# Gate vectors of the first layer on VectorE, and weight buffers with a 32-byte offset for some panels

## The chip, the cores and the metric

The kernel runs on one core of one Trainium2 chip. The metric is the device time of one execution in microseconds (us), the median of several runs. TensorE multiplies matrices, VectorE and ScalarE work on elements, GpSimd helps a little, and the queue of SyncE (SP) starts most transfers from HBM to SBUF.

## What is computed

The reference is two blocks, one behind the other, over a context of 256 tokens and a latent part of 256 tokens, each token with 1024 features, in float32.

```python
def reference(x, c, ctx, c_ctx, w_ada, b_ada, ...):
    x = first_block(x, c, ctx, c_ctx, w_ada, b_ada, g_attn, w_in, ...)
    return second_block(x, c_2, ctx_2, c_ctx_2, ada_w_2, ada_b_2, ...)
```

The first block has two layers. Each takes a modulated norm, projects it (`w_in`) into gates, latent queries and keys, and a neighbourhood attention, runs the two attentions, multiplies both by sigmoid gates, and goes through `w_out` and a feed-forward part with squared relu (`w_ff1`, `w_ff2`). The second block has two layers of one mixer each, an mLSTM and an attention with a band and a sink. In every layer shift, scale and gate vectors come from the condition: `silu(c) @ ada_w + ada_b`, for latent and context tokens. These products of a vector and a matrix are the "ada vectors".

## The kernel before

**Weights as panels.** All weights come in panels of at most 2176 columns on 128 partitions, in one order (`plan`, `items`). Most hold 8 slices of 256 columns, 1 MB. A panel is loaded into one of three raw slots (`raw`, a ring: the transfer of a panel waits until the panel before it in the slot has been used). ScalarE copies it, rounded to fp32r, into `whi` (line 1368) and VectorE writes the remainder `raw - whi` into `wlo` (line 2010), each in two halves. There are two buffers of each, so a panel's copy waits until TensorE has used the panel before the last. Activations are kept as such pairs too (XAh and XAl, and more). Each product is three fp32r matmuls: hi x hi, hi x lo, lo x hi (lines 624 to 626, and 653 to 655, 700 to 702, 718 to 720, 736 to 738 in the other forms). In `weight_left`, `weight_late`, `weight_pair` and `weight_four` the panel is the stationary operand (128 columns of it) and the activations stream, 512 columns for both token parts or 256 for one. In `tokens_left` and `tokens_half` the activations are stationary and the panel streams. A panel of 8 slices and 256 columns against 512 tokens is 2 x 8 x 3 = 48 matmuls.

**Order.** Each engine has its own program, written out by hand and in order. TensorE calls `weights(p)` and `rest(p, k)`, which wait for the first and the second half of the remainder. `begin(p)` on ScalarE and VectorE makes the hi part and the remainder of the next panel. In the gates of a layer (VectorE lines 2372 to 2395) there are four panels for each of four heads h: gm and gn (gates, 48 matmuls each in the first layer), mo and no (outputs of the two attentions, 4 slices, 24 matmuls each). VectorE multiplies the gates in, adds, and writes the remainder for the next product.

**The ada vectors.** Each vector is a row of 1024 values out of four ada panels (`ADA`, index i, four to a vector r = i // 4), each of two slices of 1024 columns. `AFTER` and `WITH` say behind which panel each stands. An ada panel uses its raw slot only. If i is not in `SUMMED`, TensorE does the product itself: `ada(i)`, 8 fp32 matmuls with 32 output partitions (line 781), each of them two records in the trace. If i is in `SUMMED`, VectorE does it (`vector_part`, line 2042): two slices, for latent and context, so four operations of 1024 columns, a product where a vector begins and a multiply-add otherwise (lines 2000 and 2005). TensorE then only adds the partitions up: `vector_sums(r)` (line 793), behind the last panel of the vector. `rows_out` moves the finished row into columns: two transposes on TensorE (line 803) and one addition on VectorE. `vector_part` stands ahead of `begin` for the same panel on VectorE, and calls `rows_out` for the second panel of a vector. Its first panel also waits for TensorE's sum of the vector before, since both use `parts_of`.

**Where tensors lie.** SBUF is allocated in the order of the program, and each tensor takes a multiple of 32 bytes per partition. The first ones (constants, small vectors, ones) end on a multiple of 64, and three of one column each (line 360) move what follows to 32 past it. So XAh, XAl, the raw slots, `whi` and `wlo` (4 x 2176 bytes each, a multiple of 64) begin at a remainder of 32 modulo 64, as every slice of a panel does. `scale1` (line 373) has 8 columns, 32 bytes, and everything behind it begins at a remainder of 0: MHL and NHL (inputs of mo and no), gYh and gYl (of wo), H (of ff2), lYh and lYl (of mw), aYh and aYl (of atw), and ckh and ckl (of ukv). Behind `gq8` (another 32 bytes) cqh and cql, the partners of uq, are at 32 again.

## Time and profile before

| | |
|---|---|
| median of 3 runs | 2008.11 us (2007.9 to 2010.7) |
| the profiled execution, its time | 2010.52 us |
| its span, first to last instruction | 2008.7 us |
| TensorE (PE) busy | 98% of the span |
| VectorE (DVE) busy | 63% |
| ScalarE (ACT) busy | 45% |
| granted clock of TensorE, mean | 0.999 |
| read from HBM | 274 MB |

The rows further down come from one profiled execution. Times are from the start of its span. PE is TensorE's matmuls, PEld its weight loads, which run beside them. A row of a matmul gives its own length with the tail of the pipeline, and the next one starts before it ends. L626 is line 626 of the kernel. In `t` and `ps` are SBUF and PSUM.

### The profile page before, as it was taken

To read this page: it belongs to the slowest core of one execution; us is meant where nothing else is said; L and a number is where in the kernel's file an instruction comes from. 1 tells how busy PE (TensorE), PEld (TensorE's weight loads), DVE (VectorE), ACT (ScalarE), POOL (GpSimd) and SP (SyncE) were. 2 spreads that over 40 slices of the span, in tenths; PEclk is the share of its full clock that TensorE was granted. 3 is DMA by queue.
4 is the path that set the end of the run, shared out by engine and by line. 5 is a ranking of instruction groups with operands and counts; after the bars stand their busy time and mean duration, and the time that the engine had idled before them with its cause. 6 is when DMAs were issued, how large, how long until landed. Compare 5 with 4: busy or idle time off the path is not lost.

```text
span 2008.7 us, 30598 instructions
## 1 busy us (share of the span) xinstructions
PE 1973.0 (98%) x12332; PEld 1649.3 (82%) x12332; DVE 1266.4 (63%) x2375; ACT 905.1 (45%) x1635; POOL 52.1 (3%) x78
## 2 busy tenths in 40 slices
PE   7999999999999999999999999999999999999998
PEld 5788777779878787899689899998887787888877
DVE  5447764546877565566665777675655464555886
ACT  4446762234423231355664554443444432234675
POOL 0000000001000000000000000000000000001000
PEclk9999999999999999999999999999999999999999
DMA  7322016443454545342129455554321133332411
GB/s 307 116 97 72 17 42 230 169 157 126 149 207 171 207 169 208 146 164 105 53 94 341 174 189 179 181 183 168 105 74 53 43 126 126 137 136 84 140 50 43
DMA packets 53580, 278.34 MB, mean 139 GB/s; under 512 B 4536, under 2 KB 19128, under 8 KB 24512
## 3 DMA queue, kind: packets, MB, share of 16 engines
q1 hardware_dynamic: 47168, 265.50, 36.5%
q10 hardware_dynamic: 6128, 10.03, 1.6%
q8 instruction: 98, 1.61, 0.3%
q0 software_dynamic: 144, 0.85, 0.1%
q14 instruction: 42, 0.34, 0.1%
HBM read 274.26 MB, written 2.11 MB: 138 GB/s over the span
## 4 chain that ended last, share of the span: by engine, by line
PE 84%; DVE 10%; ACT 3%; issue 1%; DMA 1%; POOL 0%; SPq 0%; ACTq 0%; DVEq 0%
PE ps L624 16%; PE ps L626 16%; PE ps L625 16%; PE ps L842 3%; DVE t L2010 3%; DVE t L1996 3%; PE ps L736 3%; PE ps L738 3%; PE ps L737 3%; PE ps L874 2%; PE ps L861 2%; PE ps L1234 2%; PE ps L655 2%; PE ps L653 2%; PE ps L654 2%
## 5 line engine op out<-in xcount | busy, mean ns | idle before, releaser
L624 PE MATMUL ps<-t 128*128 128x512 f32 (+1 forms) x1936 | 669.0, 346 | 3.1 <-DVE t L2010 3.1
L626 PE MATMUL ps<-t 128*128 128x512 f32 (+1 forms) x1936 | 662.6, 342 | 0.0
L625 PE MATMUL ps<-t 128*128 128x512 f32 (+1 forms) x1936 | 662.3, 342 | 0.0
L2010 DVE TENSOR_TENSOR t<-t 128x1024 fp32r<-128x1024 f32 (+2 forms) x370 | 414.2, 1160 | 197.8 <-ACT t L1368 196.9
L1368 ACT ACTIVATE t<-t 128x1024 fp32r<-128x1024 f32 (+3 forms) x376 | 357.9, 999 | 199.3 <-PE ps L626 142.9
L624 PEld LDWEIGHTS ps<-t 128*128 128x128 f32 x1936 | 365.3, 189 | 56.7 <-issue 5.9
L626 PEld LDWEIGHTS ps<-t 128*128 128x128 f32 x1936 | 365.3, 189 | 44.7
L625 PEld LDWEIGHTS ps<-t 128*128 128x128 f32 x1936 | 365.4, 189 | 43.9 <-issue 0.7
L1996 DVE TENSOR_TENSOR t<-t 128x256 f32<-128x256 f32 (+9 forms) x622 | 227.0, 386 | 141.5 <-ACT t L1740 38.1
L2005 DVE SCALAR_TENSOR_TENSOR t<-t 128x1024 f32<-128x1024 f32 (+6 forms) x340 | 234.0, 717 | 36.0 <-ACT t L1473 21.6
L1473 ACT ACTIVATE t<-ps 128x512 f32<-128x512 f32 (+2 forms) x239 | 113.6, 494 | 296.2 <-PE ps L626 198.4
L2005 DVE SCALAR_TENSOR_TENSOR t<-ps,t 128x256 f32<-128x256 f32 (+3 forms) x184 | 84.8, 483 | 133.9 <-PE ps L626 91.7
L736 PE MATMUL ps<-t 128*128 128x256 f32 (+2 forms) x524 | 158.6, 303 | 1.2 <-issue 0.7
L738 PE MATMUL ps<-t 128*128 128x256 f32 (+2 forms) x524 | 152.0, 290 | 0.0
L737 PE MATMUL ps<-t 128*128 128x256 f32 (+2 forms) x524 | 151.9, 290 | 0.0
L1996 DVE TENSOR_TENSOR t<-ps,t 128x128 fp32r<-128x128 f32 (+6 forms) x140 | 53.1, 383 | 94.6 <-ACT t L1862 34.1
L736 PEld LDWEIGHTS ps<-t 128*128 128x128 f32 x524 | 100.0, 191 | 6.9 <-issue 2.8
L737 PEld LDWEIGHTS ps<-t 128*128 128x128 f32 x524 | 100.1, 191 | 4.0 <-issue 2.4
L738 PEld LDWEIGHTS ps<-t 128*128 128x128 f32 x524 | 100.1, 191 | 1.4
L1496 ACT ACTIVATE t<-ps,t 128x512 f32<-128x512 f32 (+1 forms) x128 | 87.1, 697 | 10.5 <-DVE t L1996 10.5
L842 PE MATMUL ps<-t 64*128 64x512 f32 (+3 forms) x256 | 79.6, 571 | 0.6 <-ACT t L1473 0.6
L1485 ACT ACTIVATE t<-ps 128x1024 f32<-128x1024 f32 x56 | 57.5, 1027 | 45.9 <-PE ps L861 45.9
(191 smaller groups left out, 2349.9 us busy)
## 6 DMA issues: line engine op xcount, KB each, us to landing
t<-in_panels SPq DMA_DIRECT2D x231, 1024.0 KB, 4.9
t<-in_panels SPq DMA_DIRECT2D x12, 768.0 KB, 4.4
t<-in_panels SPq DMA_DIRECT2D x16, 512.0 KB, 4.0
t<-in_window ACTq DMA_DIRECT2D x4, 768.0 KB, 4.3
t<-gates_between ACTq DMA_DIRECT2D x4, 512.0 KB, 5.0
t<-in_panels SPq DMA_DIRECT2D x1, 1088.0 KB, 5.0
t<-in_ctxT SPq DMA_DIRECT2D x1, 1024.0 KB, 6.9
t<-in_xT SPq DMA_DIRECT2D x1, 1024.0 KB, 9.1
```

Of the source, the lines that this page charges most:

```text
L624: e.matmul(o, hi[:, k, w], xh[:, c0:c1], start=k == 0, stop=False)
L625: e.matmul(o, hi[:, k, w], xl[:, c0:c1], start=False, stop=False)
L626: t = e.matmul(o, lo[:, k, w], xh[:, c0:c1], start=False, stop=k == p.nk - 1)
L736: e.matmul(o, xh[:, r], hi[:, k, n0:n1], start=k == 0, stop=False)
L737: e.matmul(o, xh[:, r], lo[:, k, n0:n1], start=False, stop=False)
L738: t = e.matmul(o, xl[:, r], hi[:, k, n0:n1], start=False, stop=k == p.nk - 1)
L842: t = e.matmul(o[g][:, x * w:x * w + w], u["q"][g][x], u["k"][g], start=True, stop=not u["mask"])
L1368: e.activation(p.half(whi[p.buf], a), p.half(raw[p.slot], a), ACT.Copy).then_inc(*up(se, ("hi", p.i, a)))
L1473: e.activation(o, i, func, scale=scale).then_inc(*up(se, ("read", key), *names))
L1996: e.tensor_tensor(o, a, b, op).then_inc(*up(ve, *names))
L2005: e.scalar_tensor_tensor(o, a, s_, b, o1, o2).then_inc(*up(ve, *names))
L2010: e.tensor_tensor(p.half(wlo[p.buf], a), p.half(raw[p.slot], a), p.half(whi[p.buf], a).bitcast(F32), ALU.subtract).then_inc(*up(ve, ("lo", ...
```

## The change

Two things change. First, `GATES` lists gm, gn and mo of each head once, with one ada panel behind each, and all twelve (ada panels 8 to 19, the vectors 2 to 4 of the first layer) are in `SUMMED`. Before, only those behind gm were (8, 11, 14, 17), two stood behind most gn, and TensorE did the other eight. Second, `whi` and `wlo` have 2304 columns instead of 2176, and a panel's split parts begin `first_column(key)` columns in, 8 columns (32 bytes) for the panels that the function lists and 0 for the others. The raw slots stay as they are. All places that read or write `whi` and `wlo` go through `split`.

```diff
-GATES = [("gm", 0, 0), ("gn", 0, 0), ("gn", 0, 0), ("gm", 0, 1), ("gn", 0, 1), ("gn", 0, 1), ("gm", 0, 2), ("gn", 0, 2), ("mo", 0, 2),
-         ("gm", 0, 3), ("gn", 0, 3), ("gn", 0, 3)]
+GATES = [(kind, 0, h) for h in range(4) for kind in ("gm", "gn", "mo")]
...
-SUMMED = {AT_START + n for n, key in enumerate(AFTER) if key in MLP_PANELS[3:29] or len(key) == 2 or key[:2] == ("gm", 0)}
+SUMMED = {AT_START + n for n, key in enumerate(AFTER) if key in MLP_PANELS[3:29] or len(key) == 2 or key in GATES}
...
+def first_column(key):
+    kind, l, n = key[0], key[1], key[-1]
+    if kind in ("uq", "mv") or kind == "na" and n >= 4:
+        return 8
+    if (kind == "ukv" or kind in ("mo", "no") and len(key) == 3 and l == 0 or kind == "wo" and l == 0 and n < 3
+            or kind == "ff2" and l == 0 and n < 15 or kind == "mw" and n < 7):
+        return 8
+    if kind in ("cq", "ckv", "gm", "gn", "ff1") and l == 1 or kind == "ff1" and n < 2 or kind == "mq" and n < 2 or kind == "atz":
+        return 8
+    return 0
+
+
+WCOLS = 2304
...
+        self.first = 0 if self.whole else first_column(key)
+
+    def split(self, pair):
+        return pair[self.buf][:, self.first:self.first + self.nk * self.n]
...
-        whi = [sb([128, PCOLS], F32R) for _ in range(2)]
-        wlo = [sb([128, PCOLS], F32R) for _ in range(2)]
+        whi = [sb([128, WCOLS], F32R) for _ in range(2)]
+        wlo = [sb([128, WCOLS], F32R) for _ in range(2)]
...
-                hi, lo = p.view(whi[p.buf]), p.view(wlo[p.buf])
+                hi, lo = p.view(p.split(whi)), p.view(p.split(wlo))
...
-                    e.activation(p.half(whi[p.buf], a), p.half(raw[p.slot], a), ACT.Copy).then_inc(*up(se, ("hi", p.i, a)))
+                    e.activation(p.half(p.split(whi), a), p.half(raw[p.slot], a), ACT.Copy).then_inc(*up(se, ("hi", p.i, a)))
...
-                e.tensor_tensor(p.half(wlo[p.buf], a), p.half(raw[p.slot], a), p.half(whi[p.buf], a).bitcast(F32),
+                e.tensor_tensor(p.half(p.split(wlo), a), p.half(raw[p.slot], a), p.half(p.split(whi), a).bitcast(F32),
                                 ALU.subtract).then_inc(*up(ve, ("lo", p.i, a)))
```

## Rows read from the trace of the kernel before

**Rows 1.** The page: TensorE's busy time, and the chain by engine.
```profile
PE 1973.0 (98%) x12332; PEld 1649.3 (82%) x12332; DVE 1266.4 (63%) x2375; ACT 905.1 (45%) x1635; POOL 52.1 (3%) x78
...
PE 84%; DVE 10%; ACT 3%; issue 1%; DMA 1%; POOL 0%; SPq 0%; ACTq 0%; DVEq 0%
```
**Rows 2.** Timeline (start us, us, instruction): first matmuls of ff1 (0,7) and its successor.
```profile
554.14 0.39 PE L624 MATMUL ps<-t 128*128 128x512 f32 x1
...
565.02 0.40 PE L653 MATMUL ps<-t 128*128 128x512 f32 x1
```
**Rows 3.** Timeline: first matmuls of ff2 (0,7) and its successor.
```profile
690.89 0.39 PE L624 MATMUL ps<-t 128*128 128x512 f32 x1
...
702.09 0.40 PE L624 MATMUL ps<-t 128*128 128x512 f32 x1
```
**Rows 4.** Timeline: two matmuls of ukv of the first layer, twelve apart.
```profile
155.59 0.40 PE L736 MATMUL ps<-t 128*128 128x512 f32 x1
...
158.39 0.40 PE L736 MATMUL ps<-t 128*128 128x512 f32 x1
```
**Rows 5.** Timeline: first matmuls of ff1 (1,5) and its successor.
```profile
1165.90 0.28 PE L624 MATMUL ps<-t 128*128 128x256 f32 x1
...
1171.66 0.28 PE L624 MATMUL ps<-t 128*128 128x256 f32 x1
```
**Rows 6.** Timeline: first matmuls of ff2 (1,9) and its successor.
```profile
1283.14 0.28 PE L624 MATMUL ps<-t 128*128 128x256 f32 x1
...
1288.80 0.28 PE L624 MATMUL ps<-t 128*128 128x256 f32 x1
```
**Rows 7.** Timeline: first and last matmul of na (1,4), whose panel streams.
```profile
940.44 0.28 PE L736 MATMUL ps<-t 128*128 128x256 f32 x1
...
951.82 0.28 PE L738 MATMUL ps<-t 128*128 128x256 f32 x1
```
**Rows 8.** Timeline: a matmul and the weight load of the next one.
```profile
372.04 0.39 PE L624 MATMUL ps<-t 128*128 128x512 f32 x1
372.04 0.19 PEld L625 LDWEIGHTS ps<-t 128*128 128x128 f32 x1
```
**Rows 9.** Timeline of TensorE: ada blocks between panels of the first layer's gates.
```profile
303.63 0.39 PE L626 MATMUL ps<-t 128*128 128x512 f32 x1
303.94 1.95 PE L781 MATMUL ps<-t 128*32 128x256 f32 x32
305.82 0.50 PE L624 MATMUL ps<-t 128*128 128x512 f32 x1
306.16 0.39 PE L625 MATMUL ps<-t 128*128 128x512 f32 x1
...
375.53 1.07 PE L781 MATMUL ps<-t 128*32 128x256 f32 x16
376.42 1.05 PE L793 MATMUL ps<-t 128*32 128x256 f32 x16
```
**Rows 10.** Timeline of VectorE: vector parts at gm 1 and gm 2, and a remainder.
```profile
320.59 4.86 DVE L2005 SCALAR_TENSOR_TENSOR t<-t 128x1024 f32<-128x1024 f32 x4
...
357.53 1.41 DVE L2000 TENSOR_SCALAR t<-t 128x1024 f32<-128x1024 f32 x2
...
361.25 2.35 DVE L2010 TENSOR_TENSOR t<-t 128x1024 fp32r<-128x1024 f32 x2
```
**Rows 11.** Timeline of TensorE: the first matmul of gn 2.
```profile
364.56 0.39 PE L624 MATMUL ps<-t 128*128 128x512 f32 x1
```
**Rows 12.** Busy time by stretch: gates of the first, then of the second layer.
```profile
core 0: us, PE busy (x) PEld busy (x) DVE busy (x) ACT busy (x) POOL busy (x), PEclk, DMA share, GB/s
303.00:424.00 121.00, 121.00 (x657) 94.31 (x656) 55.01 (x68) 33.97 (x50) 0.00 (x0) 1.00 0.55 199
1036.00:1100.00 64.00, 63.45 (x529) 62.84 (x528) 34.69 (x55) 30.31 (x53) 0.00 (x0) 1.00 0.90 314
```
**Rows 13.** Who waited for whom from 1036 to 1240 us (total, times, longest).
```profile
PEld ps L624 <- DVE t L2010: 4.5, 7, 1.1
```
**Rows 14.** What the SP queue waited for from 280 to 430 us.
```profile
SPq L584 <- PE ps L781: 45.3, 8, 12.7
```

More of the change, by code:

```diff
@@ L643, in weight_late @@
                 o = [bank(key)[:, 0:T - c0] for key in keys]
-                hi, lo = p.view(whi[p.buf]), p.view(wlo[p.buf])
+                hi, lo = p.view(p.split(whi)), p.view(p.split(wlo))
                 for k0, k1 in ((0, 6), (6, 8)):
@@ L662, in weight_pair @@
                 o = [bank(key) for key in keys]
-                hi, lo = p.view(whi[p.buf]), p.view(wlo[p.buf])
+                hi, lo = p.view(p.split(whi)), p.view(p.split(wlo))
                 for x in parts:
@@ L690, in weight_four @@
                         xh, xl = xs(k)
-                        hi, lo = p.view(whi[p.buf]), p.view(wlo[p.buf])
+                        hi, lo = p.view(p.split(whi)), p.view(p.split(wlo))
                         if x == parts[0] and k % 4 == 0:
@@ L712, in tokens_half @@
                 o = banks(key) if k0 else bank(key)
-                hi, lo = p.view(whi[p.buf]), p.view(wlo[p.buf])
+                hi, lo = p.view(p.split(whi)), p.view(p.split(wlo))
                 r = slice(tile * 128, tile * 128 + 128)
@@ L728, in tokens_left @@
                 o = bank(key, among)[:, 0:n1 - n0]
-                hi, lo = p.view(whi[p.buf]), p.view(wlo[p.buf])
+                hi, lo = p.view(p.split(whi)), p.view(p.split(wlo))
                 r = slice(tile * 128, tile * 128 + 128)
@@ L915, in first_features @@
                     p = at["cq", 0, k // 2]
-                    hi, lo = p.view(whi[p.buf]), p.view(wlo[p.buf])
+                    hi, lo = p.view(p.split(whi)), p.view(p.split(wlo))
                     for x in ("c", "l") if k == 0 else ("cl",):
@@ L1274, in attention_layer @@
                         p = pair[k // 4]
-                        hi, lo = p.view(whi[p.buf]), p.view(wlo[p.buf])
+                        hi, lo = p.view(p.split(whi)), p.view(p.split(wlo))
                         if x == "c" and k % 4 == 0:
@@ L1327, in attention_layer @@
                     weights(p)
-                    hi, lo = p.view(whi[p.buf]), p.view(wlo[p.buf])
+                    hi, lo = p.view(p.split(whi)), p.view(p.split(wlo))
                     o = [bank(("atw", 2 * a + j))[:, 0:LAT] for j in range(2)]
@@ L2732, in lo @@
                     e.wait_ge(*done(("hi", p.i, a)))
-                    e.tensor_tensor(p.half(wlo[p.buf], a), p.half(raw[p.slot], a), p.half(whi[p.buf], a).bitcast(F32),
+                    e.tensor_tensor(p.half(p.split(wlo), a), p.half(raw[p.slot], a), p.half(p.split(whi), a).bitcast(F32),
                                     ALU.subtract).then_inc(*up(po, ("lo", p.i, a)))
```

## The prediction

> **What bounds the kernel now.** I read the engine totals and the chain of work first [rows 1]. The reader sees one core whose TensorE is busy 98% of the span, and a chain that lies on TensorE for 84%, VectorE and ScalarE together for 13%. The granted clock is 1.00 in the stretches that matter [rows 12], the level of 2.4 GHz. So an edit pays if it takes work off TensorE or makes its matmuls follow each other faster, as long as VectorE's remainders and the transfers keep up. TensorE's total is no help for the rate: a row gives a matmul of 512 columns 0.39 us, but the next starts 0.23 us later. The rate has to be read from starts.
>
> The starts show two rates for one shape. Panel ff1 (0,7) is 48 matmuls of 512 columns from 554.14 to 565.02 [rows 2]: 10.88 us, 226.7 ns each. Panel ff2 (0,7), with nothing else in between, takes from 690.89 to 702.09 [rows 3]: 11.20 us, 233.3 ns. What differs is where the operands lie. Counting the allocations (the section on the kernel does it), the ff1 panel and its activations both begin 32 bytes past a multiple of 64. For ff2 the activations are at 0 and the panel at 32. In ukv the panel streams (32) and the stationary operand is at 0: from 155.59 to 158.39 twelve matmuls start, 233.3 ns each [rows 4]. So (0,32) and (32,0) are equally slow at 512 columns and (32,32) is fast. It is the relation that counts, as far as three of the four pairs can say.
>
> At 256 columns the sign turns round. Panel ff1 (1,5), both operands at 32, takes 5.76 us for 48 [rows 5], 120.0 ns. Panel ff2 (1,9), activations at 0, takes 5.66 us [rows 6], 117.9 ns (ff2 (1,6), read the same way, 5.60 us, 116.7 ns). With the panel streaming and both at 32, 95 starts lie in 11.38 us [rows 7], 119.8 ns. A weight load runs beside each matmul, begins with it and lasts 0.19 us [rows 8], so both reads of SBUF go on at once. That makes a conflict by address possible, and it is the mechanism I assume.
>
> **Part one, the placement.** All weight buffers grow by 512 bytes, and everything behind them moves by 2048, which changes no remainder by 64. What changes it is the 32 bytes in, for the listed panels. I went through the list panel by panel. At 512 columns it names those whose partner is at 0: mo and no (8 half panels), wo 0 to 2, ff2 0 to 14, mw 0 to 6, ukv twice. With a full panel as 48 matmuls these are 4+3+15+7+2 = 31, or 1488 matmuls, and all become (0,0). At 256 columns it names those whose partner is at 32: uq, na 4 and 5, the first two of ff1, cq, ckv, gm, gn, ff1 of layer 1, mq 0 and 1, mv 1 to 7, atz, together 3396 matmuls or 70.75 times 48. They become (0,32) where the panel streams (1380) and (32,0) where it is stationary (2016). No panel on the list loses by the rates above.
> Prices for 48 matmuls: 0.32 us between the clean 512 panels, and I take 0.30, as panels behind other work show a little less. 31 x 0.30 = 9.3 us. At 256 columns 0.10 and 0.16 us are seen, I take 0.12: 70.75 x 0.12 = 8.5 us. mv 0 with its 272 columns (96 matmuls) adds 0.2. Bounds: the pair (0,0) at 512 and (32,0) at 256 stand in no row. Their nearest rows are the two rates of each shape, so (0,0) gives between -9.9 us and nothing, and if it should be a bad pair of its own the same size may be lost. I take the gain, because (0,32) and (32,0) came out equal at 512.
> Not all of that reaches the end. In the second layer's gates the transfers are busy 90% at 314 GB/s [rows 12], so gm and gn there (8 panels, 1.0 us) may only wait longer. From there to 1240 us weight loads waited seven times for VectorE's remainder, 4.5 us in all [rows 13]. ff1 panels there would give some 1.1 us. I give back 1.5 of these 2.1 us.
> The Trainium skill speaks against this half. "SBUF — State Buffer" (Who interferes with whom) says that TensorE and ScalarE "never wait on anyone", and "TensorE: Matmul & The Clock Gate" (Step-by-step: what each phase is for) that loading the next weights doesn't steal read bandwidth from the running matmul. By that the placement is worth 0 and the sum stops at part two. The rows disagree, with 226.7 against 233.3 ns at one clock.
>
> **Part two, the vectors.** ada panels 9, 10, 12, 13, 15, 16, 18 and 19 leave TensorE. Their blocks are the rows L781. The first, of two panels, starts at 303.94 and the next work at 305.82, the single one at 375.53 lasts to 376.42 [rows 9]. The three others (two, one and two panels) read the same way: 1.88, 1.86, 0.89, 1.00 and 1.75 us, together 7.38 us for eight. In the first block the spacing into it is 0.31 and behind it 0.34 us instead of 0.23, so 0.2 us more go where a block vanishes whole. Sum 7.6 us. The three sums of parts (L793) were there already and stay.
> VectorE gets 8 x 4 = 32 operations. Four multiply-adds of 1024 take 4.86 us [rows 10], so this is 39 us, placed in a stretch of 121 us where VectorE is busy 55 [rows 12]. After the change the stretch is some 112 us with up to 94 busy. It fits in sum, and I checked the order. VectorE works in order, so behind each vector part stands the remainder of the next panel, and TensorE waits for that. Today the tightest place is panel gm 2: VectorE's vector part (two short, two long operations) begins at 357.53, the remainder for gn 2 at 361.25, done 363.60, and TensorE takes it up at 364.56 [rows 10, 11], 0.96 us of slack. With four long operations it is 1.1 us later, but TensorE needs only the first half (1.2 us earlier) to start, so nothing is lost. The new parts at gn lie in a panel of 10.9 us whose remainder is ready early. The bad places are at mo. At mo 1 the part first waits for the transposes behind gn 1 (rows_out), so four operations (4.9) and half a remainder (0.65) must go into a panel of 5.55 us. At mo 2 it waits for TensorE's sum after gn 2, but has two short operations, 3.7 + 0.65. That is one stall of 0.2 to 0.3 us, and I add 0.3. DMAs: mo's transfer now waits until VectorE is done with the panel of gm, no's until the one of gn is used. That is earlier than today, where the queue waits for TensorE's ada blocks eight times, 45.3 us in all [rows 14]. So the SP queue gets no new late item. Cost at each end: 0 if the slack holds, and up to 4.9 us for every part that falls on the path.
>
> **Sum.** The profiled execution has a span of 2008.7 and a time of 2010.5 us, 2.4 above the median of the three runs, 2008.1. Rates and blocks are differences, so I set them against the median: 2008.1 - 7.6 - 9.3 - 8.5 - 0.2 + 0.3 + 1.5 = 1984.3 us.
>
> **Rivals.**
> (a) Only pairs with a row pay. (0,0) at 512 gives nothing, or (32,0) at 256, or both. That speaks for absolute positions, against it the equal rates of (0,32) and (32,0). Without the first 1993.6, without the second (42 panels, 5.0 us) 1989.3, without both 1998.6.
> (b) The placement gives nothing, since the rate hangs on something else that differs between these tensors (what wrote them, the panel before). 2008.1 - 7.6 + 0.3 = 2000.8. This is also where the skill's rule ends. Against it: the tensors at 0 are six (of mo, no, wo, ff2, mw, atw), written by different instructions, and all on the same side.
> (c) (0,0) is a bad pair of its own, and loses what it was to gain: 1984.3 + 18.6 = 2002.9.
> (d) Slower: VectorE falls behind in the first layer's gates. It decides when a remainder for the next panel ends later than TensorE's last matmul of the present one. The slack is 0.96 us now and VectorE goes from 55 to 94 us. If it never catches up, each of the eight parts lies open: 39 us of 4.9 us each, 1984.3 + 39 = 2023. For it: the six operations per mo/no pair with their round trips to ScalarE. Against it: the 10.9 us panels, gm and gn, where it catches up each time.
> (e) More than I say: clean prices for all (31 x 0.32, 70.75 x 0.16) and nothing given back, 1979.5.
>
> **How the numbers follow.** Forecast 0.66 (its own range 1981 to 1989), (a) 0.14, (b) 0.05, (c) 0.03, (d) 0.05, (e) 0.07. The range 1980 to 1996 holds the forecast, most of (a) and most of (e), about 0.8. A measurement of this kernel tells 0.2% (4 us) from no change. Faster by more: the forecast, (a), (b), (e) and a third of (c), 0.93. Within: the rest of (c) and a mild (d), 0.03. Slower 0.04.
>
> **What would show it.** ff2 (0,7) in 10.9 us instead of 11.20, ff1 (1,5) in 5.64 instead of 5.76, while ff1 (0,7) stays at 10.88. From the start of gn 0 to the start of wo 0 133.2 us shrink by 8 to 9, with L781 at 224 instead of 352 matmuls and VectorE above 80% busy. Wrong would be: equal rates at the old level (b), ff2 above 11.3 (c), waits of TensorE for VectorE's remainders of some us in the gates (d).

## The result, and the profile after

The changed kernel takes 1987.99 us (median of 4 runs, 1986.08 to 1988.45), beside 2008.43 us for the kernel before in the same comparison: a ratio of 0.9894, with a 95% interval from 0.9877 to 0.9911. Beside later kernels it came out at 1989.04 us (1986.73 to 1989.96) against 2008.5, ratio 0.9902 [0.9887, 0.9916]. The forecast was 1984.3. The span of the profiled execution is 1985.6 us instead of 2008.7, so 23.1 us less, at the same mean granted clock of 0.999 (but see the two short falls of the clock below).

The page of the changed kernel, its busy line:

```profile
PE 1948.2 (98%) x12204; PEld 1638.2 (83%) x12204; DVE 1304.7 (66%) x2407; ACT 905.0 (46%) x1635; POOL 52.2 (3%) x78
```

Against [rows 1], TensorE has 128 records fewer and is busy 24.8 us less, and VectorE has 32 operations and 38.3 us more. TensorE is still busy 98% of the span. (The chain of waits of this profile covers only 44% of the span, so I don't set it beside the 84% of before.) The matmuls of the ada blocks, L781 before, are L797 now and number 224 instead of 352:

```profile
L797 PE MATMUL ps<-t x224: 379/379/403, 462.2 to 1117.0; 128*32 128x256 f32 x112
```

**The rates**, read as before from the timeline, the first matmul of a panel and of its successor: ff1 (0,7), ff2 (0,7), ff1 (1,5), ff2 (1,9), and na (1,4), whose panel streams, with 96 matmuls.

```profile
543.27 0.39 PE L640 MATMUL ps<-t 128*128 128x512 f32 x1
554.16 0.39 PE L669 MATMUL ps<-t 128*128 128x512 f32 x1
...
678.05 0.39 PE L640 MATMUL ps<-t 128*128 128x512 f32 x1
688.93 0.39 PE L640 MATMUL ps<-t 128*128 128x512 f32 x1
...
1147.82 0.30 PE L640 MATMUL ps<-t 128*128 128x256 f32 x1
1153.52 0.29 PE L640 MATMUL ps<-t 128*128 128x256 f32 x1
...
1264.56 0.28 PE L640 MATMUL ps<-t 128*128 128x256 f32 x1
1270.16 0.28 PE L640 MATMUL ps<-t 128*128 128x256 f32 x1
...
924.58 0.28 PE L752 MATMUL ps<-t 128*128 128x256 f32 x1
935.78 0.27 PE L1041 MATMUL ps<-t 128*128 128x128 f32 x1
```

ff1 (0,7) stays at 10.89 us [rows 2]. ff2 (0,7) falls from 11.20 [rows 3] to 10.88: 226.7 ns a matmul, so (0,0) is as good as (32,32). ff1 (1,5) goes from 5.76 [rows 5] to 5.70, 118.7 ns: 0.06 us, half of what I had priced. na (1,4) has 96 in 11.20 us, 116.7 ns, where 95 took 11.38 [rows 7]. ff2 (1,9), which isn't on the list, has gone from 5.66 [rows 6] to 5.60 too.

**The gates of the first layer**, timeline of TensorE: the first matmul of gn 0 and of wo 0.

```profile
291.62 0.50 PE L640 MATMUL ps<-t 128*128 128x512 f32 x1
...
416.37 0.39 PE L669 MATMUL ps<-t 128*128 128x512 f32 x1
```

That is 124.75 us, where before it was 133.18 (the 133.2 of the prediction). Busy time of the engines in this stretch:

```profile
core 0: us, PE busy (x) PEld busy (x) DVE busy (x) ACT busy (x) POOL busy (x), PEclk, DMA share, GB/s
291.60:416.40 124.80, 124.63 (x583) 100.53 (x582) 99.66 (x110) 38.76 (x57) 0.00 (x0) 1.00 0.60 207
```

VectorE is busy 80% of it, against 55.01 of 121 us in [rows 12]. The one place where TensorE waited for it is mo 1, timeline of VectorE:

```profile
337.02 0.17 DVE L2012 TENSOR_TENSOR t<-ps,t 128x16 f32<-128x16 f32 x1 [6.26 <-PE ps L819]
337.11 4.87 DVE L2021 SCALAR_TENSOR_TENSOR t<-t 128x1024 f32<-128x1024 f32 x4
341.89 1.29 DVE L2026 TENSOR_TENSOR t<-t 128x512 fp32r<-128x512 f32 x2
```

VectorE waits for the transposes behind gn 1 (L819), does its four operations and then the remainder for no 1, whose first half ends at 342.5. TensorE started mo 1 at 336.74 and no 1 only at 342.64: 5.89 us where mo 0 took 5.47. The place and the size (some 0.3 us) are those of the forecast. In the table below this stall lies in the row of the listed 512-column panels, not in that of the ada blocks.

**All of TensorE's time by panel.** I took the distance from each matmul's start to the next one's, summed it over the panels of a kind, and set the two traces side by side. "Spacing" below is the mean distance within a panel without those over 1.15 times its median, which are waits. The differences, in us:

| | forecast | profile |
|---|---|---|
| ada blocks and other fp32 work, with gn 0 | -7.6 + 0.3 | -6.9 |
| 512 columns, listed (31 x 48 matmuls) | -9.3 | -8.3 |
| 256 columns, listed (3396 matmuls) | -8.5 + 1.5 | -5.9 |
| mv 0 | -0.2 | -0.1 |
| 256 columns, not listed (mo, no, wo, ff2 of layer 2, atw) | 0 | -1.8 |
| sum | -23.8 | -23.0 |

**Two short falls of the clock.** The first row of the table is 0.4 us short, though the stall isn't in it. Between gn 0 and wo 0 the ada blocks gave 7.7 us. But each of the two profiles has one stretch in which the granted clock stood near half, its level of 1.2 GHz, and these are different stretches: the ada blocks behind wo 3 of the second layer in the kernel before, and the work between na (1,4) and na (1,5) in the changed one. The rows are from the kernel before, from the changed kernel, and from its second profile (`after_again` below) at the same place, with the granted clock third from the end:

```profile
1130.60:1134.20 3.60, 3.60 (x40) 1.86 (x36) 3.02 (x5) 2.12 (x4) 0.00 (x0) 0.53 0.00 0
...
942.60:946.10 3.50, 3.11 (x15) 2.97 (x16) 2.27 (x6) 0.99 (x3) 0.00 (x0) 0.51 0.49 150
...
942.20:945.70 3.50, 3.08 (x28) 3.08 (x29) 3.28 (x8) 2.30 (x7) 0.00 (x0) 1.00 0.48 150
```

From the start of wo 3 to the start of ff1 0 in the second layer the kernel before took 16.4 us, and the changed one, `gates_only` and `width_only` took 15.0 to 15.1 at full clock. From na (1,4) to na (1,5) the two profiles of the changed kernel took 25.0 us with the fall and 23.5 without. So one program varies by 1.5 us from execution to execution through this alone. Whether the change makes such falls more frequent is open: in the second comparison eight of nine executions of the kernel before had a mean granted clock of 1.000, but only one of four of the changed kernel, and that one was 2.2 to 3.2 us faster than the other three (0.998 to 0.999). No pause as long as those of `dose` (below) stands ahead of either: 1.9 us at the most in the kernel before and 0.8 us in the changed one.

### The profile page after: what moved, and what is told of

Its sections match the earlier page's. It is cut to its first block and busy times, and to the rows that moved or that the text cites. A ratio compares the mean times of both kernels' runs of the same rounds, so it can differ in the third digit from the quotient of the medians.

```text
span 1985.6 us, 30374 instructions
## 1 busy us (share of the span) xinstructions
PE 1948.2 (98%) x12204; PEld 1638.2 (83%) x12204; DVE 1304.7 (66%) x2407; ACT 905.0 (46%) x1635; POOL 52.2 (3%) x78
## 5 line engine op out<-in xcount | busy, mean ns | idle before, releaser
L2021 DVE SCALAR_TENSOR_TENSOR t<-t 128x256 f32<-128x256 f32 (+4 forms) x372 | 273.1, 766 | 36.2 <-ACT t L1489 21.8
L752 PE MATMUL ps<-t 128*128 128x256 f32 (+2 forms) x524 | 156.9, 299 | 1.4 <-issue 0.7
L754 PE MATMUL ps<-t 128*128 128x256 f32 (+2 forms) x524 | 150.1, 286 | 0.0
L753 PE MATMUL ps<-t 128*128 128x256 f32 (+2 forms) x524 | 150.0, 286 | 0.0
L2016 DVE TENSOR_SCALAR t<-t 128x512 f32<-128x512 f32 (+6 forms) x177 | 74.9, 464 | 9.6 <-PE ps L809 7.0
```

The source lines that it names most:

```text
L752: e.matmul(o, xh[:, r], hi[:, k, n0:n1], start=k == 0, stop=False)
L753: e.matmul(o, xh[:, r], lo[:, k, n0:n1], start=False, stop=False)
L754: t = e.matmul(o, xl[:, r], hi[:, k, n0:n1], start=False, stop=k == p.nk - 1)
L2016: e.tensor_scalar(o, a, s1_, None, o1).then_inc(*up(ve, *names))
L2021: e.scalar_tensor_tensor(o, a, s_, b, o1, o2).then_inc(*up(ve, *names))
```

## The experiments

### The two halves apart

`gates_only` has the new order of the vectors and nothing of the placement (shown against the changed kernel, shortened; `first_column` is gone too).

```diff
 GATES = [(kind, 0, h) for h in range(4) for kind in ("gm", "gn", "mo")]
 SUMMED = {... or len(key) == 2 or key in GATES}
-whi = [sb([128, WCOLS], F32R) for _ in range(2)]
+whi = [sb([128, PCOLS], F32R) for _ in range(2)]
```

> The kernel before with the new GATES and SUMMED alone, weight buffers as before. Theory of parts: TensorE loses the eight ada blocks (7.4 us) and little else, the stretch from the start of gn 0 to the start of wo 0 goes from 133.2 to about 126 us, one stall of 0.3 us at no 1; spacing of ff2 (0,7) stays at 11.20 us for 48 matmuls. Time 2001.0 us (2000.5 to 2001.5). Rival, VectorE pays for it: waits of TensorE for remainders of more than 2 us in the gates, time above 2003.

Measured: 2001.24 us (2000.44 to 2002.26), ratio 0.996 [0.9945, 0.9975]. From gn 0 to wo 0, timeline of TensorE:

```profile
292.30 0.50 PE L623 MATMUL ps<-t 128*128 128x512 f32 x1
...
417.91 0.40 PE L652 MATMUL ps<-t 128*128 128x512 f32 x1
```

125.61 us, 7.57 less than before (forecast 7.6 - 0.3 = 7.3). No spacing of any listed kind moved by more than 0.2 ns. This half is as I had worked it out.

`place_only` has the placement with the old vectors (against the changed kernel, shortened).

```diff
-GATES = [(kind, 0, h) for h in range(4) for kind in ("gm", "gn", "mo")]
+GATES = [("gm", 0, 0), ("gn", 0, 0), ("gn", 0, 0), ("gm", 0, 1), ...]
```

> The kernel before with the 2304-column buffers and first_column alone, gate vectors as before. If the two parts only add: 2008.4 less the whole gain of the change and plus 7, about 1993 us; by panels 16.0 us less than before on TensorE. If they share a gain (TensorE waiting anyway): more than 1995.

Measured: 1996.57 us (1995.65 to 1998.94), ratio 0.9938 [0.9923, 0.9953], a gain of 12.6 us against the 2009.2 us of the kernel before in the same comparison. `gates_only` gained 8.0 there, so together 20.6, beside 20.4 for both: the halves add up. By the number the expectation missed, since 1996.6 lies where I had put a shared gain (above 1995). But its own sum, 2008.4 less 20.4 and plus 7, gives 1995 and not 1993, and its 16.0 us by panels were too many: the starts give 14.7 in this profile, whose execution was also the fastest of the four.

`width_only` has the buffers of 2304 columns, old vectors, and every panel at the first column.

```diff
-        self.first = 0 if self.whole else first_column(key)
+        self.first = 0
```

> Buffers of 2304 columns, all panels at their start (first = 0). In the changed kernel the 256-column panels that were not listed (mo, no, wo, ff2 of layer 1, atw) also became 1.8 us shorter in sum. Theory of width: the distance between the four buffers does that, so it appears here too, ff2 (1,0) to (1,14) at 116.8 ns a matmul, time 2006.6. Rival, chance or history: a block of matmuls runs in one of several steady rhythms, which one depends on how it was entered; then nothing systematic here, 2008.4 within 0.5. The listed panels keep their old spacing in both (233.3 and 119.9 ns).

Measured: 2009.28 us (10 runs, 2007.42 to 2011.19), ratio 1.0001 [0.9992, 1.0011]. The time is 0.9 us above the 2008.4 of the rival and not the 2006.6 of the theory of width, and ff2 of the second layer stays at 117.3 ns. The listed panels keep their old spacings to 0.2 ns. So the gain of the placement comes from the 8 columns alone, and the moved buffers (512 bytes wider, all behind them 2048 further) count for nothing.

### The list turned round

`mirror` puts the panels that aren't listed 8 columns in, and the listed ones at the start.

```diff
-        self.first = 0 if self.whole else first_column(key)
+        self.first = 0 if self.whole else 8 - first_column(key)
```

> Buffers of 2304 columns, and the list turned round: 8 columns for every panel that the change leaves at 0, and 0 for every listed one. Theory of relation: spacing follows whether streamed and stationary operand have the same remainder modulo 64 bytes. 2814 matmuls of 512 columns (ff1, gm, gn of layer 0, na, mk, mo, mz, cq, ckv, atkv, atq) go from 226.9 to 233.3 ns, +17 us; some 1630 of 256 columns (0,32) become (0,0), 116.7 to 119.9 ns, +4 us. Time 2029 (2026 to 2032). Rival, the tensors or what wrote them set the rate, not the remainders: 2008.4.

Measured: 2026.93 us (2025.99 to 2027.79), ratio 1.0087 [1.007, 1.0104], inside the expected 2026 to 2032. ff1 (0,7), same view as above:

```profile
560.33 0.40 PE L641 MATMUL ps<-t 128*128 128x512 f32 x1
...
571.53 0.40 PE L670 MATMUL ps<-t 128*128 128x512 f32 x1
```

The panel that was fast in both kernels, at (32,32), takes 11.20 us as (32,64). All 512-column kinds that weren't listed (ff1, gm, gn, na, mk, mo, mz, mq, atq, atkv, ckv) went from 227 or 228 to 233 ns, only cq of the first layer, whose matmuls come in short groups between others and read 231 ns before, to no more than 233, and the unlisted 256-column kinds from 116.7 to 118.0 up to 119.6 to 120.0. The same instructions on the same data get slower when only the first column moves. This rules out rival (b), by which the rate hung on what wrote the tensors.

### Which relation: modulo 64 bytes?

I had assumed that the addresses of the streamed and the stationary operand modulo 64 count. Two kernels test it with shifts that this rule can tell apart. `pad32` is the kernel before with a small tensor of 32 bytes, which moves the partners instead of the panels.

```diff
         summer, scale1 = sb([128, 32]), sb([128, 8])
+        pad = sb([128, 8])
```

> The kernel before with one more tensor of 8 columns behind scale1, so that everything behind it moves by 32 bytes; weight buffers and panels as before. All partners that were at remainder 0 are now at 32 (inputs of mo, no, wo, ff2, mw, atw, ukv), cqh and cql go to 0. Theory of relation: 1488 matmuls of 512 columns go from 233.5 to 226.9 ns, -9.5 us; 1632 matmuls of 256 columns lose 2.5 ns each, +4 us; uq (324) -0.8 us. Time about 2002. Rival, it is the position of the panel or of its buffers: no panel moved, so 2008.4.

`step64` moves the listed panels by 64 bytes instead of 32.

```diff
-        self.first = 0 if self.whole else first_column(key)
+        self.first = 0 if self.whole else 2 * first_column(key)
```

> As the placement alone, but listed panels stand 16 columns (64 bytes) in. Theory of relation modulo 64: nothing changes against the kernel with wider buffers alone, about 2006 to 2008.4, listed panels at 233.3 and 119.9 ns. Rival, any shift against the buffer's start helps (or the first bytes of a buffer are the bad ones): the gain of the change appears, 1993.

Measured: `pad32` 2001.41 us (2000.56 to 2002.49), ratio 0.9966 [0.9954, 0.9979]. The time fits the expectation, but by chance: the terms don't. At 512 columns the spacings gave 5.9 us instead of 9.5, and at 256 the panels that had been fast lost 0.6 instead of 4. ff2 (0,7) in `pad32`, then ff2 (0,7) and ff1 (1,5) in `step64`:

```profile
687.12 0.39 PE L625 MATMUL ps<-t 128*128 128x512 f32 x1
...
698.10 0.39 PE L625 MATMUL ps<-t 128*128 128x512 f32 x1
```

```profile
687.05 0.40 PE L641 MATMUL ps<-t 128*128 128x512 f32 x1
...
698.25 0.39 PE L641 MATMUL ps<-t 128*128 128x512 f32 x1
...
1157.57 0.39 PE L641 MATMUL ps<-t 128*128 128x256 f32 x1
...
1163.26 0.39 PE L641 MATMUL ps<-t 128*128 128x256 f32 x1
```

In `pad32` ff2 (0,7) takes 10.98 us, not 10.88: 229.0 ns, a value that neither kernel had. ukv, whose two operands now agree modulo 64, stays at 233.3 ns. In the second layer ff2 reads 117.8 ns where the rule wanted 119.9. `step64` misses clearly: 1999.48 us (one run) instead of 2006 to 2008. Its 512-column panels are slow as expected (11.20 us), but a shift by a whole 64 bytes, which was to do nothing at 256 columns, made ff1 faster: 114.9 ns as spacing over all of it, and cq at 113.3 ns. (ff1 (1,5), at 113.8 ns, takes 5.69 us because it also waits.) Of the 16 panels of ff1 eleven read 113.3 to 114.0 ns and five 117.7 or 117.8, with the same difference of addresses. The rule of 64 bytes falls. What holds every value so far is the streamed address minus the stationary one, modulo something larger.

### The curve over that difference

`scan` and `scan2` give single panels of ff1, ff2 and mv (in `scan2` also uq and na) first columns of their own, so that each kernel reads many differences at once. In `scan`, with the old vectors (shortened; `scan2` has the new vectors and a longer list of the same kind):

```diff
+SCAN = [0, 1, 2, 4, 6, 8, 10, 12, 14, 16, 24, 32, 40, 64, 128, 136]
...
+    if kind == "ff2" and l == 0 and n < 15:
+        return SCAN[n]
+    if kind in ("ff1", "ff2") and l == 1 and n < (16 if kind == "ff1" else 15):
+        return SCAN[n]
```

> One look at many offsets in one kernel. Gate vectors as before, listed panels at 8 columns, but ff2 of layer 0 and ff1 and ff2 of layer 1 stand at 0, 1, 2, 4, 6, 8, 10, 12, 14, 16, 24, 32, 40, 64, 128, 136 columns for their panels 0, 1, 2, ... in turn, and mv 1 to 7 at 1, 4, 8, 12, 16, 32, 64. Theory of relation modulo 64 bytes: offsets that are multiples of 16 columns give the spacing of 0, those of 8 plus multiples of 16 that of 8, and nothing depends on 512 or 1024 bytes. Offsets between 0 and 8 are unknown: a step at some column or a slope between 226.7 and 233.3 ns (512 columns), 116.7 and 119.9 ns (256). Rival, a longer period: 64 or 128 columns differ from 0.

> A second scan, with the vectors in their new order: 66 panels each get their own first column, so that the streamed address minus the stationary one, modulo 512 bytes, takes 52 further values (multiples of 4 to 48 bytes between 0 and 512), for 512 and for 256 streamed columns, and with the panel stationary or streamed. Theory now held: the spacing of the matmuls depends on that difference alone, with a period of 256 bytes (in the first scan 256 gave 120.0 ns as 0 did, 288 gave 116.7 as 32 did, and 384 gave 118.6 beside the 118.8 of 128). It expects 192 to give the 113.3 ns of 448 at 256 columns, 320 the 117.8 of 64, and at 512 columns 256 the 227 ns of 0, 192 the 233 of 448, 224 the 233 of 480, 320 the 229 of 64. Rival, period 512 bytes: 192, 320 and 256 take values of their own. With the panel streamed at 256 columns the difference 448 is to give 113.3 ns too if only the difference counts, another number if the sides are not alike. The whole: 1980 to 1990 us, since good and bad places are mixed.

Measured: 1998.61 and 1993.1 us, one run each, in which good and bad places are mixed; `scan2` lies 3 us above the 1980 to 1990 that I had given. The spacings, in ns, over the difference (streamed minus stationary address, in bytes; in brackets the same difference with 256 more, from other panels). The column for 256 is that of stationary panels, and not all differences tried are listed:

| difference | 512 columns | 256 columns |
|---|---|---|
| 0 | 226.7 to 228 (256: 226.8) | 119.9 (256: 120.0) |
| 16 | 228.3 (272: 228.9) | 119.8 (272: 119.8) |
| 32 | 233.3 (288: 233.4) | 116.7 or 117.8 (288: 116.7) |
| 48 | 232.0 (304: 231.9) | 116.7 (304: 116.7) |
| 64 | 229.0 to 229.3 (320: 229.1) | 118.0 (320: 117.7) |
| 80 | 230.0 (336: 230.0) | 118.2 (336: 118.0) |
| 96 | 233.2 (352: 233.3) | 119.9 (352: 119.9) |
| 112 | 233.3 (368: 233.3) | 120.0 (368: 119.8) |
| 160 | 234.4 (416: 234.2) | not clean (416: 120.1) |
| 192 | 233.1 (448: 233.2) | 113.7 (448: 113.3 or 117.8) |
| 224 | 233.4 (480: 233.2) | 118.2 (480: 118.4) |
| 232 | not tried (488: 230.0, 230.1) | not tried (488: 121.5, 121.7) |
| 240 | 233.3 (496: 233.4) | 118.3 (496: 118.3) |

Two readings show how such a value is taken. From `scan2`, ff2 (0,11) at a difference of 224 and ff2 (0,12) at 256, one behind the other; the third row is what follows:

```profile
771.60 0.40 PE L671 MATMUL ps<-t 128*128 128x512 f32 x1
...
782.80 0.39 PE L700 MATMUL ps<-t 128*128 128x512 f32 x1
...
793.78 0.42 PE L840 MATMUL ps<-t 128*32 128x256 f32 x4
```

11.20 us for 224 and 10.98 for 256, of which the last step, into the vectors' sum, is 0.32 instead of 0.23. From `scan`, ff1 (1,9) at 448 and ff1 (1,13) at 256:

```profile
1202.52 0.28 PE L655 MATMUL ps<-t 128*128 128x256 f32 x1
...
1208.03 0.39 PE L655 MATMUL ps<-t 128*128 128x256 f32 x1
...
1251.19 0.28 PE L655 MATMUL ps<-t 128*128 128x256 f32 x1
...
1256.95 0.28 PE L655 MATMUL ps<-t 128*128 128x256 f32 x1
```

5.51 us (with a last step of 0.19) against 5.76. Thirteen residues at 512 columns and 15 at 256 were reached both with and without 256 more, and each pair agrees within 0.6 ns. (Left out are ff1 (1,10), ff1 (1,11) and ff2 (1,4), which wait so much for VectorE that their spacing says little.) So the difference counts with a period of 256 bytes. It is no smooth curve: steps of 4 bytes change it (at 256 columns 444 reads 118.3 ns, 448 down to 113.3, 452 119.6), 512 and 256 columns like different places, and 192 may not be the only good one at 256 (436 read 113.6 in the one panel that tried it). At 512 columns nothing among the 29 residues tried beats 0.

That the difference alone counts is shown only in part. With the panel streamed, 32 gives the 116.7 ns of the stationary ff2 (uq, na, mv), 480 the 118.3, 448 and 192 the same two values, 0 the 119.9. But single panels of mv are off by up to 5 ns (112: 115.0 against 120.0, 504: 120.1 against 116, 16: 118.3 against 119.8), and in `step64`, at 64, uq of the first layer read 113.4 ns and na of the first layer 116.7 where the other streamed panels read 117.5 to 117.8. cq of the first layer, at 0, read 231 ns in all kernels that left it there, because its short groups of matmuls each begin with some longer steps. Why the period is 256, and which part of the chip makes it, no run here tells.

### Using the curve

`best1` is the changed kernel with all 256-column panels that are stationary moved to a difference of 448.

```diff
     if kind in ("cq", "ckv", "gm", "gn", "ff1") and l == 1 or kind == "ff1" and n < 2 or kind == "mq" and n < 2 or kind == "atz":
-        return 8
+        return 16
+    if (len(key) == 3 and l == 1 and kind in ("mo", "no", "wo", "ff2") or key in (("wo", 0, 3), ("ff2", 0, 15), ("mw", 7))
+            or kind == "atw"):
+        return 24
```

> The changed kernel, with the stationary panels over 256 streamed columns moved to where the scans were fastest: streamed minus stationary address 448 modulo 512 bytes (first column 16 where the other operand is at 0, 24 where it is at 32). Nothing else differs. Theory (address relation sets the spacing): 2016 matmuls from 118.4 to 113.3 ns, -10.3 us, and 1632 from 116.7 to 113.3 ns, -5.5 us, so -15.8 against the changed kernel: 1972 us (1968 to 1978, the upper end if second-layer stages then wait on other engines). Rival, that the 113.3 ns of the scans belonged to what stood around those single panels: 1983 to 1988 us.

Measured: 1983.61 us (1982.16 to 1984.02), ratio 0.9867 [0.985, 0.9883]. It is faster than the changed kernel, but by some 4 to 7 us and not by 16 (the two didn't run side by side; 4.4 by the times, 5 to 7 by the ratios to the kernel before). That is the rival's range of 1983 to 1988. The reason stands in the panels, here ff1 (1,13) and ff2 (1,9):

```profile
1238.88 0.28 PE L643 MATMUL ps<-t 128*128 128x256 f32 x1
...
1244.53 0.28 PE L643 MATMUL ps<-t 128*128 128x256 f32 x1
...
1261.30 0.28 PE L643 MATMUL ps<-t 128*128 128x256 f32 x1
...
1266.74 0.28 PE L643 MATMUL ps<-t 128*128 128x256 f32 x1
```

5.65 us and 5.44 us: 117.8 and 113.3 ns, at the same difference. Most panels at 448 have one of these two values from their first matmul to their last. In the first layer's panels and cq all have 113.3 to 113.8, in mo, no, mq, atz and atw all 117.8, and in gm, gn, wo, ff1 and ff2 both occur. A panel often keeps the value of the one before it, and changes after a wait. The two scans had hit more of the fast sort, but `step64` had already shown both values at 448, before I priced `best1` with the better one throughout.

`best2` uses 448 only where `best1` had gained, and adds uq of the first layer, streamed at 448.

```diff
+    if kind == "uq" and l == 0:
+        return 112
...
-    if kind in ("cq", "ckv", "gm", "gn", "ff1") and l == 1 or kind == "ff1" and n < 2 or kind == "mq" and n < 2 or kind == "atz":
+    if kind in ("cq", "ckv", "gn", "ff1") and l == 1 or kind == "ff1" and n < 2:
+        return 16
+    if kind == "gm" and l == 1 or kind == "mq" and n < 2 or kind == "atz":
         return 8
+    if kind == "ff2" and l == 1 or key in (("wo", 0, 3), ("ff2", 0, 15), ("mw", 7)):
+        return 24
```

> The changed kernel with the difference of 448 bytes only where it gave 113.3 ns in part of the panels, and the places of the changed kernel elsewhere: the second layer's cq, ckv, gn, ff1 and ff2, the last panels of wo and ff2 of the first layer, ff1 0 and 1, mw 7, and uq of the first layer streamed at 448. Theory: panels fall in one of two rhythms at 448 (113.3 or 117.8 ns, one for the whole panel) and in one (118.4, or 116.7 and 117.8) elsewhere. By the first version's sums per panel it gives cq -0.7, ckv -0.3, ff1 0/1 -0.9, gn -0.7, ff2 -1.6 and -0.4, wo 3 -0.1, uq -0.7, and loses ff1's +0.2: -5.2 us, 1982.8 (1980 to 1985), as fast as the first version or up to 1.5 us faster. Rival, that the rhythm a panel falls in is drawn anew by what stands before it: some panels change sides, and the sum lies anywhere between 1979 and 1987.

> The changed kernel once more, beside these two on the same chip, so that they are compared with it and not only with the one before: 1988 (1986 to 1989.5). If the rhythm of a panel is fixed by the program, its spacings by panel are those of the first profile to 0.3 ns; if it is drawn at random, the unlisted panels (116.7 or 117.8) change sides between the two profiles.

Measured side by side: `best2` 1983.1 us (1980.91 to 1985.84), ratio 0.987 [0.9854, 0.9887], the changed kernel again 1989.04 us, ratio 0.9902. So `best2` is 5.9 us faster than the changed kernel, and the same as `best1`. Its uq fell to 113.4 ns and -0.7 us as said. But cq, whose instructions and addresses are those of `best1`, changed sides, from 113.3 to 117.8 ns, and so did six panels of ff1 and ff2, in both directions. The rival was right in that panels change sides. Whether what stands before a panel in the program does it, or the single execution, these two kernels don't tell, since each was profiled once.

How much is drawn anew with each execution, the two profiles of the changed kernel show, though only for the places that it uses (0, 32, 480) and not for 448. Of 189 groups of panel and shape all but five agree within 0.7 ns. na (1,0) is off by 1 ns, and the four panels of atw change sides, here atw (1) in the first profile and in the second:

```profile
1965.33 0.28 PE L1352 MATMUL ps<-t 128*128 128x256 f32 x1
...
1970.93 0.28 PE L1352 MATMUL ps<-t 128*128 128x256 f32 x1
```

```profile
1964.12 0.28 PE L1352 MATMUL ps<-t 128*128 128x256 f32 x1
...
1969.77 0.28 PE L1352 MATMUL ps<-t 128*128 128x256 f32 x1
```

5.60 against 5.65 us, 116.7 against 117.8 ns, with one program. So in this program the rhythm is mostly fixed, and in one place it differs between executions.

### How thin the cover on VectorE is

`dose` adds two sums over 1024 elements behind each of the twelve vector parts in the first layer's gates.

```diff
+                if p.key in GATES:
+                    for k in range(2):
+                        e.tensor_reduce(scrap[:, 32 * k:32 * k + 16], w[:, k, :].rearrange("p (h e) -> p h e", e=64), AX.X,
+                                        ALU.add).then_inc(*up(ve))
                 mark(ve, ("used", a.i), ("parts", r))
```

> The changed kernel with 24 extra operations on VectorE: behind each of the twelve vector parts of the first layer's gates two sums over 1024 elements into a scratch tensor (some 1.1 us each by the 1.2 us of a remainder of 1024), and a scratch tensor of 256 bytes that moves all other operands by one period. Theory that the new order has a thin cover at mo and a thick one at gm and gn (VectorE is busy 99.7 of 124.8 us; at mo 1 TensorE is already late by 0.3 us): at the four mo panels the part grows from 4.9 to 7.1 us, and with the first half of the next remainder it no longer fits 5.5, so 2.2 us each, 4 x 2.2 = 8.8; at gm and gn 4.9 + 2.2 + 2.4 = 9.5 fits the 10.9 us. From the start of gn 0 to the start of wo 0 133 to 135 us instead of 124.8, the whole 1997 (1995 to 1999). Rival, that the stretch has spare room everywhere (126 of 125 us busy can't be quite hidden, but the queue may catch up later): 1988 to 1991. Rival, that every part comes to lie open: 24 x 1.1 = 26 more, 2014. And if the relation of addresses has the period of 256 bytes, the spacings stay 227 and 118.4 ns.

Measured: 2001.32 us (1999.99 to 2005.01), ratio 0.9964 [0.9953, 0.9976], 12.3 us above the changed kernel in the same comparison. From gn 0 to wo 0 there are 137.99 us, 13.2 more. A sum takes 1.21 us, so VectorE has 29 us more by the sums and 26.0 more by the page's busy time. Half of it came to lie open, more than I had said (133 to 135 us for the stretch, 1995 to 1999 for the whole), and not where I had said: mo 2 and mo 3 lost nothing (5.60 and 5.56 us), mo 0 and mo 1 with their neighbours lost 10, and the other 3 lie mostly behind gn 2 and in gm 3. Timeline of both engines ahead of mo 0:

```profile
291.73 1.41 DVE L2017 TENSOR_SCALAR t<-t 128x1024 f32<-128x1024 f32 x2
...
302.48 2.35 DVE L2085 TENSOR_REDUCE t<-t 128x16 f32<-128x1024 f32 x2
304.73 1.29 DVE L2027 TENSOR_TENSOR t<-t 128x512 fp32r<-128x512 f32 x2
...
305.48 0.50 PE L641 MATMUL ps<-t 128*128 128x512 f32 x1 [3.19 <-DVE t L2027]
...
306.60 0.63 PE L642 MATMUL ps<-t 128*128 128x512 f32 x1
```

VectorE comes late out of the attention: the vector part of gm 0 begins only at 291.73, when TensorE is already at gn 0. Two parts of the new length then stand ahead of the remainder for mo 0, which begins at 304.73. TensorE stands still for 3.2 us. Then comes a second price. Busy time by stretch:

```profile
core 0: us, PE busy (x) PEld busy (x) DVE busy (x) ACT busy (x) POOL busy (x), PEclk, DMA share, GB/s
303.70:305.50 1.80, 0.02 (x1) 0.03 (x1) 1.80 (x3) 0.00 (x0) 0.00 (x0) 1.00 0.00 0
305.50:308.00 2.50, 2.50 (x8) 1.95 (x9) 2.50 (x3) 0.00 (x0) 0.00 (x0) 0.69 0.83 252
```

Behind the pause the granted clock falls to a mean of 0.69, between its levels of 2.4 and 1.2 GHz. Seven matmuls of mo 0 are 427 ns apart instead of 227, with one of 303 and one of 354 around them: 1.6 us more, beside the 3.4 of the wait. The wait at the end of mo 1 (2.6 us) does the same to the first matmuls of no 1, 1.7 us. So the mechanism of rival (d) exists, and 3.3 of its 13.2 us are the clock.

The scratch tensor of 256 bytes moved all tensors behind it by one period. uq stays at 116.7, ff2 at 227.2 and 117.5 ns (in the second layer a mixture of the two rhythms, as before), as the period of 256 bytes wants.

## Why the prediction was right, point by point

- **What bounds the kernel.** Right. TensorE was and is busy 98%, and what took work from it or brought its matmuls closer came out at the end: the sums over its starts give -22.9 us (the table, and +0.1 in other panels), the span -23.1.
- **512 columns.** (0,0) was in no row, and I took the full gain because (0,32) and (32,0) were equally slow. Forecast 9.3, measured 8.3 (ff2 4.4 of 4.5, mw 2.2 of 2.1, wo 0.96 of 0.9). Missing are mo and no, which gave 0.57 of 1.2 us, and ukv, which gave 0.26 of 0.6. The price itself was right: by spacing alone the listed panels became 9.1 us shorter. mo and no lost 0.24 of theirs since their 24 matmuls begin with steps up to 236 ns behind other work (228.2 ns, not 226.7), and 0.39 in waits, the stall at mo 1 among them. ukv of the first layer only waited longer (11.85 and 11.86 us).
- **256 columns.** This is the term that was mis-sized: 5.9 instead of 8.5, or 7.0 after what I gave back. By spacing alone it is 7.3 instead of 8.5. I took 0.12 us per 48 for all, from the middle of 0.10 and 0.16. Measured are 0.15 where the panel streams (119.9 to 116.7 ns) but 0.07 where it is stationary (119.9 to 118.4). The step that failed: "(32,0)" was to be the pair of ff2. It is not. The panels of ff1 now lie at a difference of -32 (480), those of ff2 at +32, and these are two places on the curve. Modulo 64 they look alike, modulo 256 they don't.
- **Given back in the second layer.** I had put 1.5 us for gm, gn and ff1. The spacings gave 7.3 us and the panels 5.9, so 1.4 went into waits: nearly the size, but in part in other places. gm gave nothing (+0.03, where its spacing gave -0.32), ff1 0.77 of 1.21, gn all of its 0.3. The other 0.6 went in uq of the second layer (all of its 0.33), ckv, mq and mv.
- **Not listed.** I had put 0, and they gave 1.8 us: wo 0.9, ff2 0.4, atw, mo and no 0.45. `width_only` shows ff2 unmoved at 117.3 ns, so it isn't the width. These panels know two rhythms, 116.7 and 117.8 ns, and in the changed kernel more of them had the faster; that gave 1.1 us. Of wo's 0.9 only 0.16 are of this kind and the rest are waits that came and went without the change: in `width_only` wo took 22.8 us, before 23.6. That was luck, and it covered the 1.1 us that the 256 columns lacked and more.
- **The vectors.** Right in sum and place: 7.57 us by `gates_only`, one stall of 0.3 at mo 1. VectorE's cover was argued from 10.9 us panels where it catches up. `dose` shows that this holds for mo 2 and mo 3, and that the cover is used up at mo 0 and mo 1.
- **The rivals.** (b) and (c) are refuted by ff2 (0,7), (b) by `mirror` too, (a) by both shapes, though at 256 columns it came halfway. (d) did not come; with 2.4 us more on VectorE per part (`dose`) it does. (e) is off at 256 columns.
- **The Trainium skill.** The page "SBUF — State Buffer" (Who interferes with whom) of the Trainium skill has TensorE wait on nobody, and I had read that as making the placement worth nothing. It was worth 12.6 us for 8 columns, with VectorE's, ScalarE's and the queues' work unchanged. So the loss is no wait for another engine, which is what that section is about, but a cost within TensorE's own stream that it doesn't name; the reading was too wide. That the two reads of TensorE itself (streamed operand and next weights) are what meets is my reading; it agrees with the dependence on their difference, but no run took one of the reads away.

The time of 1988 lies 3.7 us above the forecast. The profile of before was 2.4 us above the median that I subtracted from, and the changed kernel's 0.2 below its own, so the same difference comes out smaller between medians. The span shrank by 23.1 us and not by 23.8 (0.7), and the time outside the span is 0.4 us longer (2.2 instead of 1.8). Of the 2.4 us some 1.3 are the fall of the clock in that one execution. The forecast had no term for the clock; how much of the changed kernel's median such falls make up, two profiles of it don't tell.

## What to carry to other kernels

Where TensorE is the bound and its matmuls come back to back, read the spacing of their starts per panel and sort it by the two operands' addresses; equal shapes with unequal spacing are the sign, and moving a buffer by a few columns is a cheap test. Test the assumed rule with shifts that it calls neutral, before using it: the kernel whose time agreed (`pad32`) had the wrong terms, and only the one that missed (`step64`) showed the better place. When work is moved to an engine that runs ahead in order, look at how late it enters the stretch, since pauses of TensorE of 2.6 and 3.2 us also cost clock behind them. Before a difference of 1 or 2 us between two profiles is explained, compare the granted clock stretch by stretch: the mean over the span, 0.999 both times, hid a fall that cost 1.5 us in one and 1.3 in the other.

## What was unexpected of the hardware

- The spacing of fp32r matmuls, each with its own weight load, depends on streamed minus stationary address modulo 256 bytes, within 0.6 ns in 28 pairs of places: 226.7 to 234.4 ns at 512 columns, 113.3 to 121.7 at 256.
- The best place for 512 columns (0, 226.7 ns) is among the worst for 256 (119.9; only 488, with 121.6, was slower in clean panels), and the best for 256 (192 or 448, 113.3 ns) is among the worst for 512 (233).
- At some differences there are two stable rhythms (113.3 and 117.8 ns at 448, 116.7 and 117.8 at 32), kept over whole panels, different between kernels with equal addresses (cq in `best1` and `best2`), and in one place (atw) between two executions of one program. What chooses them is open.
- After a pause of 3.2 us the granted clock had a mean of 0.69 over the next 2.5 us, and matmuls of 512 columns stood 427 ns apart.
- The granted clock also fell to near half (0.51 and 0.53) in stretches ahead of which TensorE had paused for 0.8 and 1.9 us at the most, and it did so in one profile of the changed kernel and not in the other.
